# HGRN scan levels in pairs: two levels per gap between projection halves, sharing the halves of two PSUM banks

## The reference, cut to what matters

```python
b = jnp.cumsum(gb, axis=2)
diff = b[:, :, :, None, :] - b[:, :, None, :, :]
decay = jnp.exp(jnp.where(mask, diff, -jnp.inf))
scores = jnp.einsum('bhtd,bhsd,bhtsd->bhts', qb, kb, decay)
```

## Time and profile before

| | us |
|---|---|
| median of 3 runs | 1464.52 |
| the 3 runs | 1464.15, 1464.52, 1466.93 |
| span of the profiled execution, first to last instruction | 1465.1 |
| PE busy in it | 1454.8 (99%) |
| DVE, ACT, POOL busy | 1197.8, 975.0, 123.3 |

### The profile page before, as it was taken

How to read it: one execution, slowest core, us unless ns; L and a number is a source line. 1 busy time by engine, 2 the same in 40 slices (tenths; PEclk the granted TensorE clock), 3 DMA queues, 4 the chain that set the end, 5 groups by cost and what they waited for, 6 DMA issues and landing times.

```text
span 1465.1 us, 20232 instructions
## 1 busy us (share of the span) xinstructions
PE 1454.8 (99%) x7509; PEld 1223.5 (84%) x7509; DVE 1197.8 (82%) x974; ACT 975.0 (67%) x894; POOL 123.3 (8%) x136
## 2 busy tenths in 40 slices
PE   9999999999999999999999999999999999999998
PEld 8978888888988888888888888888888888888886
DVE  5776766666886788888888888889888888888897
ACT  4465544445456477777777777777777777777775
POOL 5312000000222360000000000000000000000200
PEclk9999999999999899999999999999999999999999
DMA  8633985462533499999999999999999999999994
GB/s 253 227 116 117 348 282 201 156 209 82 173 115 116 149 398 396 393 381 394 376 370 395 373 369 395 388 359 391 391 369 373 395 382 370 394 381 353 399 394 171
DMA packets 210282, 450.23 MB, mean 307 GB/s; under 512 B 12940, under 2 KB 37048, under 8 KB 210232
## 3 DMA queue, kind: packets, MB, share of 16 engines
q1 hardware_dynamic: 208936, 445.09, 83.2%
q0 software_dynamic: 1152, 4.19, 0.7%
q10 hardware_dynamic: 144, 0.26, 0.0%
HBM read 435.36 MB, written 14.16 MB: 307 GB/s over the span
## 4 chain that ended last, share of the span: by engine, by line
PE 99%; ACT 0%; DVE 0%; POOL 0%; issue 0%; DVEq 0%; POOLq 0%
PE bank L1724 27%; PE bank L1726 26%; PE bank L1725 26%; PE bank L2172 5%; PE bank L2174 3%; PE bank L2221 2%; PE bank L1881 1%; PE bank L1731 1%; PE bank L2199 0%; PE bank L1921 0%; PE bank L1911 0%; PE bank L1950 0%; PE bank L2209 0%; PE bank L1744 0%; PE bank L1805 0%; PE bank L1812 0%
## 5 line engine op out<-in xcount | busy, mean ns | idle before, releaser
L1215 DVE TENSOR_TENSOR low<-raw,high 128x2048 fp32r<-128x2048 f32 x336 | 767.1, 2292 | 104.1 <-ACT high L1116 103.5
L1116 ACT CAST high<-raw 128x2048 fp32r<-128x2048 f32 x335 | 643.5, 1921 | 178.1 <-PE bank L1726 178.1
L1724 PE MATMUL bank<-high,xeh 128*128 128x512 f32 x896 | 353.5, 395 | 0.0
L1726 PE MATMUL bank<-high,xel 128*128 128x512 f32 x896 | 349.5, 390 | 0.0
L1725 PE MATMUL bank<-low,xeh 128*128 128x512 f32 x896 | 348.9, 389 | 0.0
L1726 PEld LDWEIGHTS bank<-high,xel 128*128 128x128 f32 x896 | 168.2, 188 | 35.8
L1725 PEld LDWEIGHTS bank<-low,xeh 128*128 128x128 f32 x896 | 168.4, 188 | 33.7
L1724 PEld LDWEIGHTS bank<-high,xeh 128*128 128x128 f32 x896 | 168.3, 188 | 33.5
L1724 PE MATMUL bank<-high,hdh 128*128 128x512 f32 x444 | 173.6, 391 | 0.0
L1726 PE MATMUL bank<-high,hdl 128*128 128x512 f32 x444 | 172.9, 389 | 0.0
L1725 PE MATMUL bank<-low,hdh 128*128 128x512 f32 x444 | 172.8, 389 | 0.0
(11 more groups left out here) (372 smaller groups left out, 1869.5 us busy)
## 6 DMA issues: line engine op xcount, KB each, us to landing
raw<-in_moe_w_gate_dram SPq DMA_DIRECT2D x112, 1024.0 KB, 7.5
raw<-in_moe_w_up_dram SPq DMA_DIRECT2D x112, 1024.0 KB, 8.2
raw<-in_moe_w_down_dram SPq DMA_DIRECT2D x112, 1024.0 KB, 7.9
ring<-in_w_in_dram SPq DMA_DIRECT2D x10, 2048.0 KB
dring<-in_dense_w_gate_dram SPq DMA_DIRECT2D x5, 2048.0 KB
dring<-in_dense_w_up_dram SPq DMA_DIRECT2D x5, 2048.0 KB
dring<-in_dense_w_down_dram SPq DMA_DIRECT2D x5, 2048.0 KB
ring<-in_w_in_dram SPq DMA_DIRECT2D x8, 1024.0 KB, 8.7
```

The costliest lines, as they stand in the source:

```text
L1116: act.copy(high[:, q % SPLIT, :], raw[:, q % RAW, :]).then_inc(s_hi, 1)
L1215: dve.tensor_tensor(low[:, q % SPLIT, :], raw[:, q % RAW, :], high[:, q % SPLIT, :].bitcast(F32), ALU.subtract).then_inc(s_lo, 1)
L1724: pe.matmul(o, xh, wh, start=first, stop=False)
L1726: return pe.matmul(o, xl, wh, start=False, stop=last)
```

## The change

`between()` runs level 0 in step 1 as before. It then runs two levels in each of the steps 3, 5, 7 and 9: levels 1 and 2, 3 and 4, 5 and 6, 7 and 8. Steps 2, 4, 6 and 8 have none. The odd level of a pair writes columns 0 to 255 of banks 2 and 3, the even one columns 256 to 511. The even level no longer waits for the copy of the odd one. DVE copies both after both have been multiplied, in its step of the same number. These two copies now stand ahead of `level_queries`, and so also ahead of `attn_max` in step 9.

```diff
+        def level_out(k, p):
+            return ps[2 + p][:, :] if k == 0 else ps[2 + p][:, (1 - k % 2) * SEQ:(2 - k % 2) * SEQ]
...
             def level_copy(l, k):
-                dve.wait_ge(s_lp, LEVELS * l + k + 1)
+                dve.wait_ge(s_lp, LEVELS * l + k + 1 + k % 2)
+                if k >= 2 and k % 2 == 0:
+                    dve.wait_ge(s_lc, LEVELS * l + k)
...
                     if k == 8:
                         attn_max(l, 0)
+                    if 3 <= k <= LEVELS and k % 2:
+                        level_copy(l, k - 2)
+                        level_copy(l, k - 1)
                     if 1 <= k < LEVELS:
                         level_queries(l, k)
...
-                    if 2 <= k <= LEVELS:
-                        level_copy(l, k - 1)
...
-                    pe.wait_ge(s_lc, LEVELS * l + k)
+                    pe.wait_ge(s_lc, LEVELS * l + k - (k + 1) % 2)
...
-                                ins = pe.matmul(ps[2 + p][:, w], kk[r, v], q[r, w], start=True, stop=True)
+                                o = level_out(k, p)[:, w]
+                                ins = pe.matmul(o, kk[r, v], q[r, w], start=True, stop=True)
...
                     def between():
-                        if 1 <= k <= LEVELS:
+                        if k == 1:
+                            level(l, 0)
+                        if 3 <= k <= LEVELS and k % 2:
+                            level(l, k - 2)
                             level(l, k - 1)
                         if k >= 9:
                             attn_turn(l, k - 9, 1)
```

More of the change, by code:

```diff
@@ L1277, in level_copy @@
                                                   bc(mask.unsqueeze(1), [P, 4, P // (2 * h), h]),
-                                                  ps[2 + p][:, 0:256].rearrange("p (b n m) -> p b n m", b=4, m=h))
+                                                  level_out(k, p).rearrange("p (b n m) -> p b n m", b=4, m=h))
                     elif k < 8:
@@ L1282, in level_copy @@
                     else:
-                        ins = dve.tensor_copy(SX[:, p, :, :], ps[2 + p][:, 0:256].rearrange("p (c t) -> p c t", c=2))
+                        ins = dve.tensor_copy(SX[:, p, :, :], level_out(k, p).rearrange("p (c t) -> p c t", c=2))
                 ins.then_inc(s_lc, 1)
@@ L1880, in level @@
                                 w = slice((2 * c + t) * n, (2 * c + t + 1) * n)
-                                ins = pe.matmul(ps[2 + p][:, w], kk[r, v], q[r, w], start=True, stop=True)
+                                o = level_out(k, p)[:, w]
+                                ins = pe.matmul(o, kk[r, v], q[r, w], start=True, stop=True)
                         else:
-                            ins = pe.matmul(ps[2 + p][:, c * P:(c + 1) * P], kk[r, c * SEQ:c * SEQ + P],
+                            ins = pe.matmul(level_out(k, p)[:, c * P:(c + 1) * P], kk[r, c * SEQ:c * SEQ + P],
                                             q[r, c * SEQ + P:(c + 1) * SEQ], start=True, stop=True)
```

## The result

| | before | after |
|---|---|---|
| median of the runs of the first comparison, us | 1464.41 | 1474.24 |
| ratio, 95% interval | | 1.0064 [1.0052, 1.0075] |
| the same two kernels again, on another occasion, us | 1465.50 | 1472.82 |
| ratio, 95% interval | | 1.0054 [1.0041, 1.0067] |
| span of the profiled execution, us | 1465.1 | 1474.6 |

The changed kernel is slower, by 9.8 us in the first comparison and by 7.3 us in the second. The changed kernel's profiled execution took 1476.39 us as a run, 1.8 us more than its span. The kernel before has a run, 1466.93 us, that lies as far above its span of 1465.1. So that was probably its profiled execution, and the span stood 0.6 us above the median only because it was the longest of the three. Beside the second comparison one run of the kernel before took 3737.53 us; nothing here explains it, and the ratio leaves it out.

What follows compares the result with a forecast made beforehand. PE was taken as the bound, with 99% of the chain of waits. Per layer -0.57, -1.27 + 1.25 and +1.08 + 2.15 give +2.64; 1464.5 + 5.3 (two layers) + 0.9 (clock) = 1470.7 us, range 1467.0 to 1473.8.

Steps and rivals of the forecast that it cites:

- both waits: PE waits for ACT at the second scores in step 8, 1.25 us, and the first attention product in step 9, 2.15 us.
- Pairs: Levels (1,2), (3,4), (5,6) each pay entry and exit once, saving 0.19 us a pair: -0.57 us a layer.
- Steps 3, 5, 7 at no cost: DVE's delayed copies and the work queued behind them cost 0; up to 0.5 us a layer if the cover were gone.
- The reading in which the copies block too: Step 7: DVE's copies also block against POOL's key multiplication, making it 0.2 us late a layer; not used in the sum.
- Step 8, saving lost: Removing level 7 saves PE 1.27 us, but waiting for group 0's exponentials adds 1.25 us: net 0.
- Step 9: Level 7 adds 1.08 us; group 1's maxima, queued behind four copies, make PE wait 2.15 us at the first attention product.
- Step 10: Second such chain: copy of turned weights at 119.8, PE at 119.95; nothing added, 0.1 us to spare.
- The clock: PE standing still 2.15 us may bring the half-speed clock once a layer: +0.9 us taken, bounds 0 and 3.4.
- the one spell in two behind the four-row matmuls: Nearest profile row for the clock: half-speed stretch in one case of two, costing 1.7 us, in layer 1 only.
- more than the sum: Rival: clock falls in both layers (1473.2 us), or step 10's cover is missing (about 1472); chance 0.2.

Runs made afterwards that it cites:

- six levels in pairs: Changed kernel with levels 7 and 8 back in steps 8 and 9, copies and maxima in the old order there: 1463.48 us against 1465.50 for the kernel before.
- no level 7: Kernel before with 15 of level 7's 16 matmuls left out: 1465.84 us against 1465.78 for the kernel before.
- Maxima first: Changed kernel with attn_max of group 1 put back ahead of the two level copies in DVE's step 9: 1465.06 us against 1465.50 for the kernel before.
- before, maxima late: Kernel before with the copy of level 8 moved ahead of attn_max of group 1 in DVE's step 9: 1468.55 us against 1465.78 for the kernel before.
- filled kernel: Changed kernel with ten 512-column matmuls in PE's queue just before each layer's first attention product: 1469.81 us against 1465.50 for the kernel before.
- only the first maxima early: Changed kernel with only group 0's maxima moved ahead of the low weights of half 11, in DVE's step 7: 1469.03 us against 1465.78 for the kernel before.
- both maxima early: Changed kernel, group 1's maxima ahead of the two copies, group 0's in DVE's step 7 ahead of the low weights: 1461.48 us, again 1460.19; before 1465.78, 1465.77.

## Why the prediction was right, and what it missed

The direction and both waits were right. The time was forecast at 1470.7 with a range up to 1473.8. The first comparison gave 1474.2, 0.4 us above the range, the second 1472.8, inside it. The term that was mis-sized is the clock's, and the pairs saved more than forecast; the two errors work against each other, so that the sum came as near as it did is in part luck.

- **Pairs.** 0.19 us saved was forecast, 0.37 measured. The step had taken only the gaps at entry and exit of the level's group. The level matmuls themselves come closer together in a pair too, 1.98 us for 32 against 2 x 1.08.
- **Steps 3, 5, 7 at no cost.** Right. In step 7 DVE waits 1.83 us for the cast, more than the 1.43 of before though two more copies stand ahead; "six levels in pairs" confirms it with 1.19 us saved per layer. The spare time was larger than the 0.5 to 1 us forecast because of POOL. Step 7 on POOL and DVE, first the kernel before, then the changed one:

```profile
...
86.39 1.29 POOL L787 TENSOR_TENSOR KDk<-HK,DX 128x512 f32<-128x512 f32 x1 [6.70 <-ACT DX L987]
...
86.51 1.45 DVE L1262 TENSOR_TENSOR QD<-HQ,DX 128x256 f32<-128x256 f32 x1
...
87.12 1.30 POOL L791 TENSOR_TENSOR KDk<-HK,DX 128x512 f32<-128x512 f32 x1 [6.27 <-ACT DX L991]
...
87.02 1.66 DVE L1282 COPY_PREDICATED SC<-LM,bank 128x256 f32<-128x256 int32 x4
88.57 0.42 DVE L1266 TENSOR_TENSOR QD<-HQ,DX 128x256 f32<-128x256 f32 x1
...
```

Before, the queries stood beside POOL's multiplication and took 1.45 us. Now the four copies stand there, take 1.66 us together and are not held up, and the queries behind them take 0.42 us. The reading in which the copies block too is out.

- **Step 8, saving lost.** Right: 1.24 us of wait against the 1.25 forecast, and "no level 7" shows it by itself.
- **Step 9.** Forecast +1.08 and 2.15 us of wait; measured 0.94 and 2.28. The sum, 3.23 against 3.22, is right since what the shorter pair saves turns into wait. "Maxima first" and "before, maxima late" show from both sides that the order on DVE makes it.
- **Step 10.** Right: the second product starts 0.32 us after the last projection matmul, as before, 122.22 against 121.90. Here the spell had made PE late, and the copy ended 1.7 us ahead of it (120.54). In the filled kernel, which has no spell, the copy ended at 117.52 and PE came at 117.66: 0.14 us to spare, where 0.1 was forecast.
- **The clock.** This is the term that was mis-sized: +0.9 forecast, +4.5 in the profiled execution. A spell cost 1.5 us and not 1.7, but there were three more and not half of one. Two spells followed the two long waits. Of six waits of that length in all (both layers of the changed kernel, of its repeat, and of the one with only the first maxima early) five were followed by a spell. The step that failed was to take this from the one spell in two behind the four-row matmuls, where PE had not stood still, and to halve it again for the spell that might go; that one stayed, at 398 us. The rival "more than the sum" had a spell in both layers, as 1473.2. The third extra spell, at 60 us in layer 0, comes and goes between executions of one kernel: it was absent in the repeat, and the kernel with both maxima early had it in one of two profiled executions.

Forecast without the clock +5.3, measured +4.1 us; the clock +0.9 against +4.5, both in the profiled execution. How the 9.8 and 7.3 us of the medians divide is not shown.

## What to carry to other kernels

A reordering that saves a gap on the busiest engine also moves instructions on the engines that feed it. Follow every instruction that is now queued behind the moved one, up to who waits for it: here two pairs of copies of 0.8 us a pair, which themselves wait for the moved matmuls, stood ahead of a reduction, and the wait cost more (2 x 2.28 us) than eight gaps saved (8 x 0.37). The cure was to put the instruction that heads the chain to PE (the row maxima) ahead of the work with slack; only then did all four pairs pay. And compare stretches of the profile with equal numbers of half-clock spells: here a layer's time then repeats to 0.1 us, where the medians of the changed kernel moved by 1.4 us and the runs of one kernel spread over up to 7.

## What the runs showed of the hardware

- A wait of 2.3 us on PE, with 1 us of small attention matmuls behind it, was followed by a fall of the granted clock from full to half (2.4 to 1.2 GHz) in five of six cases, at 1.5 us each. After waits of 1.4 us there was none in two, after waits filled with matmuls none in two, and where the wait was missing none in 16. The stretch of 2 us with four-row matmuls had one in 12 of 24 passes over the kernels that have it whole, with PE not idle, and not in the same ones when a kernel ran again.
- In the kernel with both maxima early, the negation of eight numbers per partition took 1.25 us, where the same one took 0.17 in the changed kernel (at 95.02). POOL's multiplication of the keys ran from 89.60 to 90.89, and DVE's small operation, which started at 89.66, ended at 90.91. The Trainium skill, "SBUF — State Buffer", in "Who interferes with whom", says that a DVE operation in a two-port mode is fully blocked by a GpSimd operation that was issued first, and names `tensor_scalar` among those that can run in such a mode. The trace agrees with the blocking; the mode itself stands in no view. DVE's row stands above (89.66); POOL's, on that kernel's timeline, is:

```profile
...
89.60 1.29 POOL L791 TENSOR_TENSOR KDk<-HK,DX 128x512 f32<-128x512 f32 x1 [4.31 <-ACT DX L991]
...
```
